# Scores of a gated recurrent branch: float32 products replaced by three products of rounded high and low parts, in a two-block transformer kernel

## The chip, the cores and the metric

The kernel is one program on one core of a Trainium2 chip. The metric is device time in microseconds (us) of the whole program. Its engines are TensorE (PE in the profile; PEld is its weight load), VectorE (DVE), ScalarE (ACT), GpSimd (POOL) and SyncE (SP), which issues most transfers.

## The reference, cut to what matters

The first of two blocks has two layers (`l` = 0, 1) over 256 context tokens and 256 latent tokens. Each layer has three branches. The first, A, is a gated linear-attention recurrence with 4 heads, 128 wide in queries and keys and 256 wide in values, run forwards and backwards. In one chunk of the reference:

```python
qh = heads(q, A_QK)
kh = heads(k, A_QK) * (A_QK ** -0.5)
a = jnp.exp(dmat - m_row[..., None]) * jnp.einsum('bhtd,bhsd->bhts', qc, kc)
num = jnp.einsum('bhts,bhsv->bhtv', a, vc) + ...
den = jnp.sum(a, axis=-1) + ...
h = num / jnp.maximum(jnp.abs(den), jnp.exp(-m_row))[..., None]
```

The change touches only how `q k^T` is multiplied. Everything is float32 in the reference.

## The kernel before

**Split products.** Nearly all matrix products of the kernel are made as three products of rounded parts: x = high + low, where high is x rounded to the type `fp32r` and low is x - high rounded to it, and xy is taken as high·high + high·low + low·high (`mm3`). Weights arrive by DMA in units of up to 128x2048 in `raw`. ScalarE writes the high part of a unit (`wh`), in a first piece of 1280 and a second of 768 columns, and VectorE writes the low part (`wl`) in the same two pieces. In the code this conversion is `used(tag, j)`: it converts the unit two turns later in the order, because there are two buffers, and it can start only when TensorE has finished the unit that it replaces. So `used("a_qk", ...)` stands behind the keys' projection.

**Branch A.** Tokens lie in four tiles of 128. Layer 0 computes all four (N = 512 queries); layer 1 computes the last two (N = 256 queries) against all 512 keys. For head `h` TensorE goes through, in this order:

- the query projection into PSUM bank 0 and the key projection into bank 1 (`queries`, `keys`; for head 0, `first_units`);
- at heads 0 and 2, values of two heads (`values_of`), tile by tile into banks 0, 1, 2, 3 (head 0 of layer 1: banks 4, 5, 0, 1);
- turning the output of the head before (`outputs_turned`), and at odd heads the first half of the output gate (`o_gate(h, (0,))`, bank 0);
- the scores, one product per tile of queries into banks 4 to 7: 256 keys for tiles 0 and 1, 512 keys for tiles 2 and 3. They are plain float32 products of `a_qk`;
- the rest of the output gate, the `z` gate, the turning of the weighted scores (`turns`) and the product with the values (`outs`).

ScalarE copies bank 0 and bank 1 to `a_qk` (events `a_q`, `a_k`), and its copy of the keys carries the scale. These copies also free the banks: `values_of` and `o_gate` wait for them. Scores of layer 0 wait besides for the end of the previous head's output on VectorE (`a_y`).

**VectorE's order.** Each engine runs its instructions strictly in the order written. At the end of a head, VectorE does `root`, `diagonals(h + 1)`, the low part of the unit behind `a_qk` (`used`), `outputs(l, h)` and then, in the next head, the score multiplications (`tensor_tensor_reduce`). Before head 0 it makes the gates' running sums: a memset, six scans, four small operations (event `a_rc`). ScalarE then stores the factors to memory and reads them back spread over all partitions (`factors_stored`, `factors_spread`), VectorE adds them up in `diagonals(0)`, ScalarE takes the exponentials (`exponentials(0)`) and, in layer 0, only then copies the values out of banks 0 to 3 (event `a_v`). The first output gate of layer 0 waits for that copy, because it writes bank 0.

Of the kernel before, what the change touches and what calls it, by code (L numbers as in the profile page):

```python
# [11 lines left out]
ALU = mybir.AluOpType  # L12
ACT = mybir.ActivationFunctionType
# [208 lines left out]
def program(nc, wpk, xin, memt, vec, tabs, tabs2, rpb, out):  # L222
# [13 lines left out]
    with ctx:  # L236
# [3 lines left out]
        def signal(name):  # L240
            return Signal(name, ctx.enter_context(nc.semaphore(name)))
# [31 lines left out]
        act_step = signal("act_step")  # L273
        lo_split = signal("lo_split")
        dve_step = signal("dve_step")
# [27 lines left out]
        def tm(off, shape):  # L303
            n = int(np.prod(shape))
            v = TM[:, off:off + n]
            if len(shape) == 2:
                v = v.rearrange("p (a b) -> p a b", a=shape[0])
            elif len(shape) == 3:
                v = v.rearrange("p (a b c) -> p a b c", a=shape[0], b=shape[1])
            return v  # L310

        def bank(b):
            return PS[:, b]
# [4 lines left out]
        def hy(base, kn, n):  # L318

            parts = HY[:, :, base:base + kn * n].rearrange("p s (k t) -> p s k t", k=kn)  # L320
            return parts[:, 0], parts[:, 1], parts
# [43 lines left out]
        YB = hy(4096, 8, 512)  # L365
# [16 lines left out]
        GROUPS = ((0, 0), (1, 256))  # L382


        a_qk, a_f, a_b = tm(0, [2, 512]), tm(2048, [4, 512]), tm(4096, [4, 512])
        a_v, a_v_pair = [tm(o, [4, 256]) for o in (1024, 6144)], tm(0, [2, 5120])[:, :, 1024:2048]
        a_dirs = (a_f, a_b)
        a_g, a_z, a_h, a_rr = tm(7168, [2, 512]), tm(8192, [2, 512]), tm(9216, [4, 256]), tm(9216, [2, 512])
# [259 lines left out]
        def tensor_program(P):  # L648
            free = {}

            def mm(o, l, r, start=True, stop=True):
                return P.x.matmul(o, l, r, start=start, stop=stop)  # L652
# [156 lines left out]
            def branch_a(l):  # L809
                t0, N = lay(l)  # L810
# [36 lines left out]
                def values_of(h, half, tiles):  # L847
                    u = place["a_v", 4 * l + h + half]
                    w, v = weights(u)
                    for i in tiles:  # L850
                        o = a_v_bank(l, h, i)
                        if half == 0 and o < 2:
                            P.wait_ge(act_step, (("a_q", "a_k")[o], l, h))
                        elif half == 0 and o == 2 and h == 0:
                            P.wait_ge(act_step, ("a_gt", l))
                        for k in range(4):
                            split_done(u, k)
                            P.wait_ge(*ready(4 * half + k))
                            t = mm3(bank(o), H[0][:, 4 * half + k, 128 * i:128 * i + 128], H[1][:, 4 * half + k, 128 * i:128 * i + 128],
                                    w[:, k], v[:, k], half == 0 and k == 0, half == 1 and k == 3)  # L860
                        if half or i == 3:
                            t.then_inc(*projected.mark(*([("a_v", l, h, i)] if half else []), *([("unit", u)] if i == 3 else [])))
# [21 lines left out]
                def o_gate(h, cs):  # L884
                    u = place["a_o", 4 * l + h]
                    for c in cs:
                        if h % 2:
                            P.wait_ge(act_step, (("a_q", "a_k")[c], l, h))
                        else:
                            P.wait_ge(act_step, ("a_v", l, h, c + 2 if l and h == 0 else c))  # L890
                        proj_t(bank(c)[:, 0:N], u, 128 * c, 128, H, ready, 0, 8, t0, N, ("a_o", l, h, c), *([("unit", u)] if c else []))
# [21 lines left out]
                for h in range(4):  # L913
                    if h % 2:
                        o_gate(h, (0,))
                    P.wait_ge(act_step, ("a_k", l, h))
                    if h == 0:
                        P.wait_ge(act_step, ("a_cm", l))
                    elif l == 0:
                        P.wait_ge(dve_step, ("a_y", l, h - 1, 1))  # L920
                    for i in range(i0, 4):
                        n = a_keys(i)
                        mm(bank(4 + i)[:, 0:n], a_qk[:, 0, 128 * i:128 * i + 128], a_qk[:, 1, 0:n]).then_inc(
                            *pe_step.mark(("a_s", l, h, i)))
                    o_gate(h, (1,) if h % 2 else (0, 1))
                    u = place["a_z", 4 * l + h]
                    for c in range(2):
                        P.wait_ge(act_step, ("a_o", l, h, c))
                        proj_t(bank(c)[:, 0:N], u, 128 * c, 128, H, ready, 0, 8, t0, N, ("a_z", l, h, c), *([("unit", u)] if c else []))
                        if c == 0:  # L930
                            turns(h)
                    outs(h)
                    if h < 3:
                        queries(h + 1)
                        keys(h + 1)
                        if h == 1:
                            values_of(2, 0, (0, 1))
                        outputs_turned(l, h)
                    if h == 1:
                        values_of(2, 0, (2, 3))  # L940
                        values_of(2, 1, range(4))
# [819 lines left out]
        def scalar_program(A):  # L1761
            def act(o, i, f, *events, **kw):
                return A.x.activation(o, i, f, **kw).then_inc(*act_step.mark(*events))  # L1763
# [59 lines left out]
            def branch_a(l):  # L1823
                t0, N = lay(l)
# [18 lines left out]

                def queries(h):
                    A.wait_ge(projected, ("a_q", l, h))
                    act(a_qk[:, 0, t0:512], bank(0)[:, 0:N], ACT.Copy, ("a_q", l, h))

                def keys(h):
                    A.wait_ge(projected, ("a_k", l, h))
                    act(a_qk[:, 1], bank(1), ACT.Copy, ("a_k", l, h), scale=128.0 ** -0.5)  # L1850
                    used("a_qk", 4 * l + h)

                def values_of(h, tiles):
# [647 lines left out]
            for l in range(2):  # L2501
                t0, N = lay(l)
# [38 lines left out]
        def vector_program(D):  # L2541
            def tt(o, a, b, op, *events):
                return D.x.tensor_tensor(o, a, b, op).then_inc(*dve_step.mark(*events))  # L2543
# [6 lines left out]
            def stt(o, a, s, b, op0, op1, *events):  # L2550
                return D.x.scalar_tensor_tensor(out=o, in0=a, scalar=s, in1=b, op0=op0, op1=op1).then_inc(*dve_step.mark(*events))  # L2551
# [14 lines left out]
            def used(tag, j):  # L2566
                convert(unit_after(place[tag, j]))
# [78 lines left out]
            def ada_turn(q):  # L2646
                l, j = divmod(ada_content(q), 12)
                D.wait_ge(pe_step, ("ada_turned", q))
                groups = bank(turn_bank(q))[:, 0:256].rearrange("p (h g c) -> p h c g", h=2, g=4)[:, :, 0:2]
                D.x.reduce_sum(group_sums, groups, AX).then_inc(*dve_step.mark())  # L2650
                D.wait_own(dve_step)
                tt(ada[:, l, 2 * j:2 * j + 2, :], group_sums, vcol(f"bada{l}", 2 * j, 2).unsqueeze(2).to_broadcast([128, 2, 2]), ALU.add, ("ada", q))
# [43 lines left out]
            def branch_a(l):  # L2696
                t0, N = lay(l)
                i0 = t0 // 128
                used("gate", l)
                if l:  # L2700
                    used("a_qk", 4)
                    ada_turn(23)
                D.wait_ge(act_step, ("a_ln", l))
                stt(a_g[:, 1], a_gt, 0.0, a_g[:, 0], ALU.min, ALU.subtract)
                D.wait_own(dve_step)
                cp(a_fg[0], a_g[64:68, 1])
                cp(a_fg[1], a_g[96:100, 1])
                D.x.memset(a_z[:, 1], 0.0).then_inc(*dve_step.mark())
                D.wait_own(dve_step)

                def scan(o, a, b, init, op):
# [21 lines left out]
                def diagonals(h):  # L2733
                    if h:
                        D.wait_ge(pe_step, ("a_turned", l, h - 1, 3))
                    D.wait_ge(factors_in[h % 2], (l, h))
                    for d in range(2):
                        for i in range(i0, 4):
                            a0 = 128 * i
                            stt(a_dirs[d][:, i, a0:a0 + 128], a_factor(d, h)[:, a0:a0 + 128], a_col(d, i, h), a_masks[d],  # L2740
                                ALU.add, ALU.add, ("a_diag", l, h, d))

                diagonals(0)
                for h in range(4):
# [51 lines left out]
                    root(colS[:, 28 + i0:32], colS[:, 20 + i0:24], colS[:, 24 + i0:28], ("a_root", l, h), eps=64 * EPS)  # L2796
                    if h < 3:
                        diagonals(h + 1)
                        used("a_qk", 4 * l + h + 1)
                        outputs(l, h)  # L2800
                        if h == 1:
                            outputs_low(l, 1)

# [6 lines left out]
            def outputs(l, h):  # L2810
                t0, N = lay(l)
                for c in range(2):
                    D.wait_ge(pe_step, ("a_yt", l, h, c))
                    stt(a_z[:, c, 0:N], bank(4 + c)[:, 0:N], vcol(f"anw{l}", 2 * h + c), a_g[:, c, 0:N], ALU.mult, ALU.mult, ("a_y", l, h, c))
# [1131 lines left out]
```

## Time and profile before

| | us |
|---|---|
| median of 3 runs | 2233.77 (2231.61 to 2234.32) |
| the profiled execution | 2233.6 |
| its span, first to last instruction | 2231.6 |
| PE busy | 2208.0 (99%) |
| PE weight loads busy | 1955.8 (88%) |
| DVE busy | 1367.8 (61%) |
| ACT busy | 1046.8 (47%) |
| POOL busy | 275.1 (12%) |

Busy time is the union of an engine's instructions. The times of single rows below count from the first instruction of the span. A matmul's row lasts longer than its turn on the engine, as successive ones overlap: the step from one start to the next is what it costs.

### The profile page before, as it was taken

The page shows a single profiled execution, that of the slowest core. Times are in us where ns is not written, and L with a number is a line of the kernel's source. Part 1 is how long each engine was busy: PE and PEld are TensorE (multiplying, and loading weights), DVE is VectorE, ACT ScalarE, POOL GpSimd, SP SyncE. Part 2 cuts the span into 40 slices and gives each one's busy share as a digit, 9 for nine tenths or more (in the row PEclk, how much of TensorE's full clock was granted, in tenths as well). Part 3 has the DMA queues.
Part 4 walks back from the last instruction along what each step waited for, and adds up shares of the span by engine and source line. Part 5 has one row for each costly group of instructions (what it writes and reads, how often), then busy time and mean ns, then how long its engine had stood idle before and what let it go on. Part 6 is the DMA issues. An engine that isn't in the chain of part 4 may idle for free.

```text
span 2231.6 us, 35053 instructions
## 1 busy us (share of the span) xinstructions
PE 2208.0 (99%) x14494; PEld 1955.8 (88%) x14494; DVE 1367.8 (61%) x2620; ACT 1046.8 (47%) x1994; POOL 275.1 (12%) x299
## 2 busy tenths in 40 slices
PE   8999999999999999999999999999999999999998
PEld 7888878999978888878899999999888888988887
DVE  6644523577755243467465776557777876667875
ACT  5543422345442233354443556445466554566553
POOL 0000000222201032100002220120210110110110
PEclk9999999999999999999999999999999999999999
DMA  8522234221234222235343223446433555334544
GB/s 314 185 96 77 76 151 170 77 77 58 77 107 141 93 78 93 85 132 172 112 151 133 79 93 114 178 166 218 147 124 136 190 178 191 119 107 142 186 174 147
DMA packets 55535, 298.09 MB, mean 134 GB/s; under 512 B 9344, under 2 KB 16256, under 8 KB 24208
## 3 DMA queue, kind: packets, MB, share of 16 engines
q1 hardware_dynamic: 53040, 291.62, 37.0%
q10 hardware_dynamic: 2336, 4.23, 0.7%
q8 instruction: 114, 1.87, 0.3%
q14 instruction: 45, 0.37, 0.0%
HBM read 292.65 MB, written 3.44 MB: 133 GB/s over the span
## 4 chain that ended last, share of the span: by engine, by line
PE 90%; DVE 6%; ACT 2%; DMA 1%; issue 1%; POOL 0%; SPq 0%; DVEq 0%; ACTq 0%
PE PS L652 86%; PE PS L656 3%; DVE TM L2543 1%; DVE wl L2562 1%; ACT TM L1763 1%; ACT TMG L1763 0%; DVE wl L2564 0%; DVE colS L2551 0%; DVE colS L3146 0%; ACT wh L1773 0%; DMA raw<-in_wpk 0%; DVE TMG L2551 0%; DMA Y<-factors_d 0%; DVE HY L2551 0%; ACT HY L1763 0%
## 5 line engine op out<-in xcount | busy, mean ns | idle before, releaser
L652 PE MATMUL PS<-HY,wh 128*128 128x512 f32 (+3 forms) x4944 | 1282.3, 343 | 5.8 <-DVE TM L2551 1.7
L652 PEld LDWEIGHTS PS<-HY,wh 128*128 128x128 f32 (+2 forms) x4944 | 847.9, 189 | 122.3 <-issue 9.4
L652 PE MATMUL PS<-HY,wl 128*128 128x256 f32 (+1 forms) x3000 | 925.2, 308 | 0.0
L652 PEld LDWEIGHTS PS<-HY,wl 128*128 128x128 f32 x3000 | 566.8, 189 | 30.0
L2562 DVE TENSOR_TENSOR wl<-raw,wh 128x1280 fp32r<-128x1280 f32 (+1 forms) x238 | 346.9, 1458 | 362.8 <-ACT wh L1773 362.7
L652 PE MATMUL PS<-wh,HY 128*128 128x256 f32 (+1 forms) x2468 | 527.3, 306 | 0.2
L1763 ACT ACTIVATE TM<-PS 128x512 f32<-128x512 f32 (+4 forms) x375 | 184.2, 500 | 520.1 <-PE PS L652 416.9
L652 PEld LDWEIGHTS PS<-wh,HY 128*128 128x128 f32 x2468 | 405.8, 191 | 19.7 <-ACT TM L1763 0.8
L1773 ACT ACTIVATE wh<-raw 128x1280 fp32r<-128x1280 f32 (+2 forms) x246 | 295.8, 1202 | 243.6 <-PE PS L652 171.8
L652 PE MATMUL PS<-wl,HY 128*128 128x256 f32 (+1 forms) x1234 | 373.4, 303 | 0.0
L2564 DVE TENSOR_TENSOR wl<-raw,wh 128x768 fp32r<-128x768 f32 (+1 forms) x238 | 249.8, 1049 | 0.0
L652 PEld LDWEIGHTS PS<-wl,HY 128*128 128x128 f32 x1234 | 236.1, 191 | 8.6
L1774 ACT ACTIVATE wh<-raw 128x768 fp32r<-128x768 f32 (+2 forms) x246 | 200.2, 814 | 0.0
L3518 POOL TENSOR_TENSOR HY<-TM,HY 128x256 fp32r<-128x256 f32 (+2 forms) x64 | 62.7, 981 | 351.2 <-ACT HY L1763 350.3
L1763 ACT ACTIVATE TMG<-PS 128x512 f32<-128x512 f32 (+2 forms) x113 | 49.3, 457 | 105.9 <-PE PS L652 98.6
L2543 DVE TENSOR_TENSOR TM<-PS,TM 128x512 f32<-128x512 f32 (+3 forms) x92 | 47.6, 545 | 72.5 <-ACT TM L1763 70.2
L1763 ACT ACTIVATE TMG<-PS,colS 128x512 f32<-128x512 f32 (+1 forms) x108 | 63.9, 599 | 57.0 <-DVE colS L2547 56.4
L652 PE MATMUL PS<-TM 128*128 128x128 f32 (+4 forms) x512 | 86.7, 331 | 1.0 <-ACT TM L1763 0.7
L3518 POOL TENSOR_TENSOR TM<-TM,wtab 128x256 f32<-128x256 f32 x64 | 68.2, 1086 | 74.1 <-DVE colS L2907 67.6
L3518 POOL TENSOR_TENSOR TM<-TM,T 128x512 f32<-128x512 f32 (+2 forms) x30 | 30.9, 1046 | 371.3 <-PE PS L652 188.9
L652 PEld LDWEIGHTS PS<-TM 128*128 128x128 f32 (+2 forms) x512 | 65.9, 190 | 9.4 <-issue 5.0
L1763 ACT ACTIVATE HY<-TM 128x256 fp32r<-128x256 f32 (+2 forms) x82 | 42.1, 520 | 60.2 <-POOL TM L3518 31.5
(198 smaller groups left out, 1798.7 us busy)
## 6 DMA issues: line engine op xcount, KB each, us to landing
raw<-in_wpk SPq DMA_DIRECT2D x233, 1024.0 KB, 4.8
raw<-in_wpk SPq DMA_DIRECT2D x32, 704.0 KB, 4.0
TM<-in_wpk SPq DMA_DIRECT2D x6, 1024.0 KB, 16.7
Y<-factors_d ACTq DMA_DIRECT2D x16, 256.0 KB, 5.5
X<-in_xin SPq DMA_DIRECT2D x1, 2048.0 KB, 15.3
Y<-in_wpk SPq DMA_DIRECT2D x2, 1024.0 KB, 20.5
Y<-bias_d SPq DMA_DIRECT2D x4, 512.0 KB, 10.2
raw<-in_wpk SPq DMA_DIRECT2D x3, 512.0 KB, 3.7
```

The lines of the kernel that those rows point to most:

```text
L652: return P.x.matmul(o, l, r, start=start, stop=stop)
L656: return P.x.transpose(o, i, ident[0:p, 0:p])
L1763: return A.x.activation(o, i, f, **kw).then_inc(*act_step.mark(*events))
L1773: A.x.activation(wh[:, s, 0:c], raw[:, r, 0:c], ACT.Copy).then_inc(*hi_split.mark((u, 0)))
L1774: A.x.activation(wh[:, s, c:n], raw[:, r, c:n], ACT.Copy).then_inc(*hi_split.mark((u, 1)))
L2543: return D.x.tensor_tensor(o, a, b, op).then_inc(*dve_step.mark(*events))
L2562: D.x.tensor_tensor(wl[:, s, 0:c], raw[:, r, 0:c], wh[:, s, 0:c], ALU.subtract).then_inc(*lo_split.mark((u, 0)))
L2564: D.x.tensor_tensor(wl[:, s, c:n], raw[:, r, c:n], wh[:, s, c:n], ALU.subtract).then_inc(*lo_split.mark(u))
L3518: return G.x.tensor_tensor(o, a, b, op).then_inc(*pool_step.mark(*events))
```

## The change

Queries and keys of branch A are no longer kept as float32 in `a_qk`. ScalarE's two copies now write rounded high parts into a slice of the `fp32r` buffer `YB` (`a_high(0)` for queries, `a_high(1)` for keys), and VectorE makes the low parts (`a_low`) from the PSUM banks and the high parts: `low_queries` one tensor-tensor subtraction, `low_keys` one scalar-tensor-tensor operation with the scale. Each score product becomes three. What waited for ScalarE's copies in order to overwrite banks 0 and 1 now waits for the low parts, and the scores wait for both low parts. VectorE's new operations stand: for head 0 ahead of the gate work (layer 1) or ahead of the scans (layer 0); for later heads, the queries' behind `diagonals(h + 1)`, and the keys' behind the conversion `used("a_qk", ...)` at h + 1 = 2, and behind `outputs(l, h)` as well at h + 1 = 1 and 3.

```diff
-        a_qk, a_f, a_b = tm(0, [2, 512]), tm(2048, [4, 512]), tm(4096, [4, 512])
+        a_f, a_b = tm(2048, [4, 512]), tm(4096, [4, 512])
+
+        def a_high(c):
+            return YB[c][:, 6]
+
+        def a_low(c):
+            return YB[c][:, 7]
...
                         if half == 0 and o < 2:
-                            P.wait_ge(act_step, (("a_q", "a_k")[o], l, h))
+                            P.wait_ge(dve_step, ("a_low", l, h, o))
...
                         if h % 2:
-                            P.wait_ge(act_step, (("a_q", "a_k")[c], l, h))
+                            P.wait_ge(dve_step, ("a_low", l, h, c))
...
                     P.wait_ge(act_step, ("a_k", l, h))
+                    P.wait_ge(dve_step, ("a_low", l, h, 0), ("a_low", l, h, 1))
...
-                        mm(bank(4 + i)[:, 0:n], a_qk[:, 0, 128 * i:128 * i + 128], a_qk[:, 1, 0:n]).then_inc(
+                        own = slice(128 * i, 128 * i + 128)
+                        mm3(bank(4 + i)[:, 0:n], a_high(0)[:, own], a_low(0)[:, own], a_high(1)[:, 0:n], a_low(1)[:, 0:n], True, True).then_inc(
                             *pe_step.mark(("a_s", l, h, i)))
...
-                    act(a_qk[:, 0, t0:512], bank(0)[:, 0:N], ACT.Copy, ("a_q", l, h))
+                    act(a_high(0)[:, t0:512], bank(0)[:, 0:N], ACT.Copy, ("a_q", l, h))
...
-                    act(a_qk[:, 1], bank(1), ACT.Copy, ("a_k", l, h), scale=128.0 ** -0.5)
+                    act(a_high(1), bank(1), ACT.Copy, ("a_k", l, h), scale=128.0 ** -0.5)
                     used("a_qk", 4 * l + h)
...
+                def low_queries(h):
+                    D.wait_ge(act_step, ("a_q", l, h))
+                    tt(a_low(0)[:, t0:512], bank(0)[:, 0:N], a_high(0)[:, t0:512], ALU.subtract, ("a_low", l, h, 0))
+
+                def low_keys(h):
+                    D.wait_ge(act_step, ("a_k", l, h))
+                    stt(a_low(1), bank(1), 128.0 ** -0.5, a_high(1), ALU.mult, ALU.subtract, ("a_low", l, h, 1))
+
+                if l:
+                    low_queries(0)
+                    low_keys(0)
                 D.wait_ge(act_step, ("a_ln", l))
...
                 D.x.memset(a_z[:, 1], 0.0).then_inc(*dve_step.mark())
+                if l == 0:
+                    low_queries(0)
+                    low_keys(0)
                 D.wait_own(dve_step)
...
                         diagonals(h + 1)
+                        low_queries(h + 1)
                         used("a_qk", 4 * l + h + 1)
+                        if h == 1:
+                            low_keys(h + 1)
                         outputs(l, h)
+                        if h != 1:
+                            low_keys(h + 1)
```

## Rows read from the trace of the kernel before

**Rows 1.** The page: TensorE's granted clock in 40 slices, 9 for 90% or more.

```profile
PEclk9999999999999999999999999999999999999999
```

**Rows 2.** The page: the chain of work that ended last, by engine.

```profile
PE 90%; DVE 6%; ACT 2%; DMA 1%; issue 1%; POOL 0%; SPq 0%; DVEq 0%; ACTq 0%
```

**Rows 3.** Timeline, float32 scores, layer 0 head 0: start, us, engine, line, operation.

```profile
97.19 2.74 PE L652 MATMUL PS<-TM 128*128 128x256 f32 x8
...
99.77 0.19 PEld L652 LDWEIGHTS PS<-HY,wh 128*128 128x128 f32 x1 [0.24 <-issue]
```

**Rows 4.** Timeline, TensorE: split products 512 and 256 columns wide.

```profile
182.56 0.39 PE L652 MATMUL PS<-wl,HY 128*128 128x512 f32 x1
...
183.24 0.39 PE L652 MATMUL PS<-wl,HY 128*128 128x512 f32 x1
...
1041.39 0.28 PE L652 MATMUL PS<-HY,wl 128*128 128x256 f32 x1
...
1041.75 0.28 PE L652 MATMUL PS<-HY,wl 128*128 128x256 f32 x1
```

**Rows 5.** Timeline, layer 0, VectorE's outputs ahead of the scores of head 1, and the scores.

```profile
143.24 1.41 DVE L2551 SCALAR_TENSOR_TENSOR TM<-PS,V,TM 128x512 f32<-128x512 f32 x2
...
145.32 2.74 PE L652 MATMUL PS<-TM 128*128 128x256 f32 x8
```

**Rows 6.** Timeline, layer 0 before and at head 0: weight loads, ScalarE, VectorE.

```profile
73.52 1.28 ACT L1763 ACTIVATE TM<-PS 128x512 f32<-128x512 f32 x2 [3.21 <-PE PS L652]
...
74.17 0.19 PEld L652 LDWEIGHTS PS<-wh,HY 128*128 128x128 f32 x1 [0.43 <-ACT TM L1763]
74.28 0.19 PEld L652 LDWEIGHTS PS<-wl,HY 128*128 128x128 f32 x1
...
72.63 1.21 DVE L2712 TENSOR_TENSOR_SCAN TM<-TM 4x512 f32<-4x512 f32 x1
...
80.18 0.67 DVE L2543 TENSOR_TENSOR rows<-TMG,TM 4x512 f32<-4x512 f32 x1
...
82.90 2.13 ACTq L1842 DMA_DIRECT2D Y<-factors_d  x4
...
92.46 2.19 DVE L2551 SCALAR_TENSOR_TENSOR TM<-Y,colC,T 128x128 f32<-128x128 f32 x8 [5.62 <-DMA Y<-factors_d]
...
98.32 2.07 ACT L1763 ACTIVATE TM<-PS 128x512 f32<-128x512 f32 x4 [0.89 <-ACT TM L1763]
```

**Rows 7.** Timeline, layer 0, keys of head 2 and the values behind them.

```profile
181.66 0.39 PE L652 MATMUL PS<-wh,HY 128*128 128x512 f32 x1
...
184.15 0.61 PE L652 MATMUL PS<-wh,HY 128*128 128x512 f32 x2
...
181.85 0.60 ACT L1763 ACTIVATE TM<-PS 128x512 f32<-128x512 f32 x1 [1.23 <-PE PS L652]
...
185.06 0.95 DVE L2564 TENSOR_TENSOR wl<-raw,wh 128x768 fp32r<-128x768 f32 x1
```

**Rows 8.** Timeline, layer 1, keys and scores of head 1.

```profile
1042.95 1.88 PE L652 MATMUL PS<-TM 128*128 128x512 f32 x4
...
1043.91 0.87 DVE L2551 SCALAR_TENSOR_TENSOR TM<-PS,V,TM 128x256 f32<-128x256 f32 x2
1044.70 0.55 DVE L2756 CUSTOM_DVE_ANT_0 TM<-PS,TM 128x384 f32<-128x384 f32 x1
```

**Rows 9.** Timeline, layer 1, TensorE at the gates of head 0.

```profile
1023.82 1.32 PE L656 MATMUL PS<-T,TM 128*128 128x128 f32 x8 [0.20 <-DVE TM L2551]
```

**Rows 10.** Windows at the end of the span: TensorE busy (instructions), granted clock, DMA share, GB/s.

```profile
2226.00:2228.00 2.00, 0.00 (x1) 1.00 0.16 54
2228.00:2230.00 2.00, 0.00 (x0) 0.64 1.03 340
```

**Rows 11.** Waits of TensorE from 1140 us to the end: us, times, longest; 9 rows, first and last.

```profile
PE PS L652 <- DVE TM L2551: 1.7, 1, 1.7
...
PE PS L656 <- DVE colS L2551: 0.2, 1, 0.2
```

## The prediction

> **What bounds the kernel now.** I read the page first, for the bound: the chain that ended last is TensorE for 90% of the span [rows 2], and its granted clock is full in every slice [rows 1]. So an edit counts in two ways only: by the time that its own products take on TensorE, and by the time that TensorE is held at a wait. Then I read timelines around the eight places where scores are made (four heads in each of two layers), to see what TensorE does in the moments in which it will have to wait for VectorE. The question at each place: when does the new low part come, and when does TensorE want it?
>
> **What the products save.** Eight matmul records make the four float32 scores of a head of layer 0. They begin at 97.19, and the weight load that starts with the first gate product's turn is at 99.77 [rows 3]: 2.58 us for 256+256+512+512 columns, or 1.68 ns a column, so 0.86 for 512 and 0.43 for 256. Split products step by 0.68 us for three at 512 columns (182.56 to 183.24) and by 0.36 for three at 256 (1041.39 to 1041.75) [rows 4]. A head of layer 0 then takes 2×0.68 + 2×0.36 = 2.08: 0.50 less. A head of layer 1, with two products of 512, takes 1.36 instead of 1.72: 0.36 less. All eight heads: 3.4 us. That is all that can be won, and less than the 4.5 us (0.2%) that a measurement of this kernel can tell from no change.
>
> **What is added.** ScalarE's copies stay as they are, with another output. VectorE gets sixteen operations. The nearest price is two operations of 128x512 with a PSUM operand in 1.41 us, 0.70 each [rows 5]; the writing to the rounded type is not shown with a PSUM operand, so I bound it from both sides: not under half of that, 0.35, as the data are the same, and not over twice, 1.4. I take 0.70. VectorE has the time. What matters is that it works in order, and what stands ahead of the keys' low part. One more price: a wait that truly holds TensorE also stops its weight loads from running ahead. At 74.17 a load was released and the next one started at 74.28 [rows 6], so the first product begins 0.11 after its release.
>
> **Values of heads 2 (once in each layer), the first large cost.** The first tile of values goes to bank 0 from 181.66; the second starts at 184.38, the second product of the row at 184.15 (0.23 later) [rows 7], and it goes to bank 1. It used to need ScalarE's copy of the keys, which starts at 181.85 and takes 0.60 [rows 7]: long done. Now it needs `low_keys`, and ahead of that on VectorE stands the conversion of the unit whose buffer the keys' projection has only just left: ScalarE rounds it behind the copy, VectorE follows, and its last piece runs from 185.06 for 0.95 [rows 7]. So `low_keys` runs from 186.01 to 186.71, the product starts at 186.82, and TensorE is held 2.44 us. In layer 1 the same chain stands behind the same product, with the same distances. Two places: 4.9. Behind the held product stand TensorE's whole queue and all that follows it; nothing takes up the time.
>
> **Scores of heads 1 and 3 in layer 1, the second.** They begin at 1042.95 and waited for no VectorE result. The conversion and both outputs now stand ahead of `low_keys`: the outputs begin at 1043.91, and what followed them began at 1044.70 [rows 8]. So `low_keys` ends at 1045.40, the scores start at 1045.51, and TensorE is held 2.56. The pattern repeats at head 3. Two places: 5.1. The score multiplications that began at 1044.70 shift by less than TensorE does, so no second wait comes of it.
>
> **Scores of heads 1 and 3 in layer 0.** Here N is twice as large and covers it: the outputs run from 143.24 for 1.41, `low_keys` would end at 145.35, and the scores began at 145.32 [rows 5]. With the 0.11, 0.14 at most; I take 0.1, twice: 0.2.
>
> **Head 0 of layer 0.** Two things. The first tile of values was released at 74.17 by the copy of the queries [rows 6] and now waits 0.70 more for `low_queries`. And the scans: they started at 72.63, while TensorE was still projecting; now they stand behind `low_keys`, which waits for the copy of the keys (73.52 + 1.28 = 74.80 [rows 6]) and ends at 75.5. The scans, the factors (last operation at 80.18), the store, the spreading read (issued from 82.90) and the sums that wait for it (92.46, idle until the transfer landed) all move by 2.9 [rows 6]. ScalarE works without a pause worth the name from there to its copies of the values, whose first starts at 98.32 [rows 6] and, with the 0.60 of such a copy [rows 7], ends at 98.92. Moved, 101.82; with the 0.11, 101.93. The first gate began at 99.77 [rows 3] and needs that bank, so it is late by 2.16. This is counted from before, so the 0.70 and the head's own saving are in it.
>
> **Head 0 of layer 1.** VectorE's two operations stand where it waits for ScalarE, and two other tiles go first, so I cost them at nothing; without that cover they would cost up to 1.4. But its saving of 0.36 is lost too: soon after these scores TensorE waits for VectorE's weights (0.20 at 1023.82 [rows 9]), which hang on the spread factors and not on TensorE, and it would only wait longer.
>
> **The sum.** Held: 2.16 + 4.88 + 5.12 + 0.2 = 12.4. Saved: 3×0.50 + 3×0.36 = 2.6. Net +9.8. On the profiled execution's 2233.6 (the median of the runs is 2233.77, the same for this purpose) that is 2243.4.
>
> **Rival 1: the factors are not late.** The spreading read takes long: issued from 82.90, the last that counts landed before 92.46, 9.6 us on [rows 6], beside a weight unit on the same engines. Moved by 2.9, it could meet less traffic and land relatively earlier. For it: the lag is long. Against it: that unit is released by VectorE's next conversion, which moves by the same amount. If all 2.9 are regained, the first gate is late only by 0.70 - 0.50 = 0.2, the net is 7.8 and the time 2241.4. Chance 0.08.
>
> **Rival 2: the clock falls in the new pauses.** TensorE has no pause of over 1.7 us in the later part of the run [rows 11], and its clock, 2.4 GHz, is full throughout [rows 1]. After its last work, which ended by 2226.00, it did nothing more, and in the window from 2228 to 2230 the mean granted clock is 0.64, on the way to 1.2 GHz [rows 10]. The four long pauses, 2.3 to 2.5 us, lie between what these rows show at full clock and what they show at its fall. If it fell, the products behind would go at half speed for a while; I bound that by nothing and by two lengths of the pause, so 0 to 2.4 us lost each time. One fall: up to 2245.8; four: up to 2253. Chance of at least one: 0.12. The Trainium skill ("TensorE: Matmul & The Clock Gate", HAM oscillation) says that an engine which idles between bursts is throttled and must work its way back to full rate. By that rule these pauses, not the waits alone, would be the cost; the trace shows full rate through its longest pause, and so I keep the sum without it.
>
> **Rival 3, the other side: the time is given back later, and no change can be measured.** While TensorE is held, ScalarE, VectorE and the transfers could get ahead, and TensorE's later waits would shrink. From 1140 us on there are nine kinds of them, from 1.7 down to 0.2 and 6.3 us in all [rows 11]. If all went, the net is 3.5, and the time 2237.1, within 4.5 of before; it decides from 5.3 of the 6.3. Against it: such waits are steps of dependent chains (a sum, its root, its spreading) that begin with TensorE's own product and so move with it. Chance 0.06.
>
> **How the numbers follow.** Forecast 0.70, rivals 0.08, 0.12 and 0.06; 0.04 is left for what I do not see, half of it for a score product that runs better than the rows say, so that the kernel is faster. The likeliest case has its own range: the VectorE operation at 0.35 takes about 0.35 off each of the five large terms, at 1.4 it adds 0.7 to each, and near 0.7 it is well supported; 2241.5 to 2246. The range of 8 in 10 takes in rival 1 and one fall of the clock: 2240 to 2248. Slower: 0.70 + 0.08 + 0.12 + 0.01 = 0.91; within 0.2%: 0.06 + 0.01 = 0.07; faster 0.02.
>
> **What would show each step.** In the profile after: three split products per score at 0.68 and 0.36 us; TensorE idle, put down to VectorE, about 2.4 us in the middle of the values of head 2 in both layers and about 2.5 before the scores of heads 1 and 3 in layer 1; the scans of layer 0 starting near 75.5 and the first gate near 101.9, put down to ScalarE; no wait before the scores of layer 0's heads 1 and 3 beyond 0.14; the granted clock at full in all slices. The prediction is wrong if `low_keys` takes much more or less than 0.70, if the clock falls, or if the factors land early.

## The result, and the profile after

| | before | changed |
|---|---|---|
| median, us | 2233.85 (2231.61 to 2236.65, 6 runs) | 2244.28 (2242.84 to 2247.2, 6 runs) |
| ratio | | 1.0053 [1.0043, 1.0063] |
| the profiled execution, its span | 2233.6, 2231.6 | 2247.2, 2245.4 |

The changed kernel is slower by 10.4 us (2244.28 − 2233.85); 9.8 were forecast (2243.4 us). Its profiled execution is the slowest of its six runs, 13.6 over before's, so the trace below has some 3 us more to explain than the median.

The page of the changed kernel: busy times, and the chain that ended last, by engine. They answer to [rows 2].

```profile
PE 2211.1 (98%) x14518; PEld 1962.8 (87%) x14518; DVE 1378.3 (61%) x2636; ACT 1046.9 (47%) x1994; POOL 274.0 (12%) x299
...
PE 88%; DVE 7%; ACT 3%; DMA 1%; issue 1%; ACTq 0%; POOL 0%; SPq 0%; DVEq 0%
```

VectorE is busy 10.5 us more than before and TensorE 3 us more, and the chain has moved 2% of the span from TensorE to VectorE and ScalarE. The clock line of its page is that of [rows 1], 9 everywhere, which says only that no slice of 56 us fell below 90%: a fall of a few microseconds does not show in it. Where TensorE waits says more.

TensorE's waits in the changed kernel between 60 and 1160 us (total us, times, longest):

```profile
PE PS L659 <- DVE HY L2560: 5.3, 5, 2.1
PE PS L659 <- ACT HY L1772: 4.8, 2, 2.4
...
PE PS L659 <- DVE HY L2552: 0.7, 1, 0.7
```

The first line has two waits of 2.1 us for `low_keys` (line 2560 writing `HY`) among its five; the other three, 1.0 us in all, wait for other work of that line and were there before. The last is `low_queries` of head 0. The second line looks like ScalarE, and the timeline shows that it is not.

Timelines of the changed kernel, layer 1, VectorE, ScalarE and TensorE around the scores of head 1 (they answer to [rows 8]):

```profile
1048.57 0.95 DVE L2573 TENSOR_TENSOR wl<-raw,wh 128x768 fp32r<-128x768 f32 x1
1049.44 0.87 DVE L2560 SCALAR_TENSOR_TENSOR TM<-PS,V,TM 128x256 f32<-128x256 f32 x2
1050.23 0.68 DVE L2560 SCALAR_TENSOR_TENSOR HY<-PS,HY 128x512 fp32r<-128x512 f32 x1
...
1050.34 0.63 ACT L1772 ACTIVATE HY<-TM 128x512 fp32r<-128x512 f32 x1 [2.48 <-DVE TM L2560]
...
1048.36 0.28 PE L659 MATMUL PS<-HY,wl 128*128 128x256 f32 x1
1051.05 2.30 PE L659 MATMUL PS<-HY 128*128 128x512 f32 x6 [2.42 <-ACT HY L1772]
```

In this order VectorE makes the second piece of a weight unit, two outputs, and only then `low_keys`, which ends at 1050.91. The score products wait for `low_keys` by the program. ScalarE's copy of the outputs, to another part of `HY`, happens to end at 1050.97, 0.06 later, and the profile puts a wait down to what ended last. TensorE was to begin at 1048.48 (1048.36 plus the step of 0.12) and begins at 1051.05: 2.57 us held.

The same for the values of head 2 in layer 0 (they answer to [rows 7]):

```profile
185.87 0.95 DVE L2573 TENSOR_TENSOR wl<-raw,wh 128x768 fp32r<-128x768 f32 x1
186.74 0.68 DVE L2560 SCALAR_TENSOR_TENSOR HY<-PS,HY 128x512 fp32r<-128x512 f32 x1
...
184.96 0.39 PE L659 MATMUL PS<-wh,HY 128*128 128x512 f32 x1
187.47 0.50 PE L659 MATMUL PS<-wh,HY 128*128 128x512 f32 x1 [2.13 <-DVE HY L2560]
187.81 0.39 PE L659 MATMUL PS<-wl,HY 128*128 128x512 f32 x1
...
188.76 0.63 PE L659 MATMUL PS<-wl,HY 128*128 128x512 f32 x1
190.04 0.63 PE L659 MATMUL PS<-wl,HY 128*128 128x512 f32 x1
```

Without a wait the next product would begin at 185.19. It is released at 187.47, and the product behind it starts 0.34 later instead of 0.23, so the first itself begins at 187.58: held 2.39 us. The same `x6 [2.42` comes back at 1131.42, and the same 2.13 at 1080.35: four pauses, as foreseen. The last two rows were not foreseen as the likely course: from one product with `wl` to the next is 1.28 us instead of 0.68 [rows 4].

TensorE in five stretches of the changed kernel: stretch, us, busy (matmuls), mean granted clock, DMA share, GB/s. The first four us of work behind each of the four pauses, and the stretch around 975.

```profile
188.00:192.00 4.00, 4.00 (x12) 0.57 0.68 247
973.00:977.00 4.00, 4.00 (x24) 0.57 0.41 172
1051.00:1055.00 4.00, 3.95 (x15) 0.60 0.57 231
1080.00:1084.00 4.00, 3.65 (x18) 1.00 0.74 262
1131.00:1135.00 4.00, 3.58 (x24) 1.00 0.65 246
```

The clock is at 1.2 GHz for most of the first three stretches and at 2.4 GHz in the last two. So two of the four pauses of this execution were followed by a fall, two were not, and one fall, at 973, stands behind no long pause. Before the change no slice of the page fell below 90% [rows 1], and windows of its trace from 60 to 1160 and from 1160 to 2226 us have a mean of 1.00.

Head 0 of layer 0, VectorE, ScalarE, TensorE (they answer to [rows 6] and [rows 3]):

```profile
74.98 0.69 DVE L2560 SCALAR_TENSOR_TENSOR HY<-PS,HY 128x512 fp32r<-128x512 f32 x1
75.71 1.21 DVE L2736 TENSOR_TENSOR_SCAN TM<-TM 4x512 f32<-4x512 f32 x1
...
94.33 2.19 DVE L2560 SCALAR_TENSOR_TENSOR TM<-Y,colC,T 128x128 f32<-128x128 f32 x8 [6.62 <-DMA Y<-factors_d]
...
85.76 1.85 ACTq L1851 DMA_DIRECT2D Y<-factors_d  x4
...
100.84 0.73 PE L659 MATMUL PS<-HY,wh 128*128 128x512 f32 x2 [0.53 <-ACT TM L1772]
```

The scans start late by 3.1 us and the read is issued late by 2.86, but the sums that wait for it start late by only 1.87: 8.57 us lie between them, against 9.56 before. The gate's second weight load, which stood at 99.77 before [rows 3], is at 100.94: late by 1.17, where 2.16 were forecast. The other profiles of kernels with this order (experiments 1 to 4) have 8.64 to 9.12 us between the two, and the gate late by 1.1 to 1.8.

**The ledger of this trace** compares the start of the same product in both traces, in us: first gate +1.17; held values of heads 2, 2×2.4; held scores of heads 1 and 3 of layer 1, 2×2.57; the saving and small waits of the other heads, −2.3; the clock falls at 188 and 1051, 1.6 each, and at 973, 0.5; and 1.1 at 842, told below. That makes 13.6, and the last product is late by 13.7.

### The profile page after: what moved, and what is told of

Same layout as the page of the kernel before. It is cut to its first block, busy times and chain, and to the rows that moved or that the text cites. A ratio compares the mean times of both kernels' runs of the same rounds, so it can differ in the third digit from the quotient of the medians.

```text
span 2245.4 us, 35118 instructions
## 1 busy us (share of the span) xinstructions
PE 2211.1 (98%) x14518; PEld 1962.8 (87%) x14518; DVE 1378.3 (61%) x2636; ACT 1046.9 (47%) x1994; POOL 274.0 (12%) x299
## 3 DMA queue, kind: packets, MB, share of 16 engines
q8 instruction: 114, 1.87, 0.3%
## 4 chain that ended last, share of the span: by engine, by line
PE 88%; DVE 7%; ACT 3%; DMA 1%; issue 1%; ACTq 0%; POOL 0%; SPq 0%; DVEq 0%
PE PS L659 84%; PE PS L663 3%; DVE TM L2552 1%; DVE wl L2571 1%; ACT TM L1772 1%; DVE wl L2573 1%; DMA Y<-factors_d 1%; ACT wh L1782 1%; ACT TMG L1772 0%; DVE TM L2736 0%; ACT HY L1772 0%; DVE colS L3175 0%; DVE colS L2560 0%; DMA raw<-in_wpk 0%; DVE HY L2560 0%
## 5 line engine op out<-in xcount | busy, mean ns | idle before, releaser
L1772 ACT ACTIVATE TM<-PS 128x512 f32<-128x512 f32 (+3 forms) x359 | 175.5, 498 | 505.1 <-PE PS L659 403.5
L2552 DVE TENSOR_TENSOR TM<-TM 128x256 f32<-128x256 f32 (+7 forms) x146 | 65.7, 465 | 5.9 <-POOL TM L3547 1.2
L659 PE MATMUL PS<-TM 128*128 128x128 f32 (+3 forms) x464 | 68.2, 312 | 1.0 <-ACT TM L1772 0.7
```

## The experiments

Every kernel is compared with runs of the kernel before in its own group. Experiments 1, 2, 3 and the ten products of 4 were run in one group (before: median 2234.13 of 18 runs), the others in a second (2232.81 of 15). The changed kernel itself was run in the second, and in the first measurement above (before: 2233.85), but not in the first group. Line numbers of helpers move by some lines between kernels.

**1. The low part of the keys at the head of the queue.** Products, copies and waits stay as changed; heads 1 to 3 lose their place behind the weight conversion and the outputs.

```diff
                         low_queries(h + 1)
+                        low_keys(h + 1)
                         used("a_qk", 4 * l + h + 1)
-                        if h == 1:
-                            low_keys(h + 1)
                         outputs(l, h)
-                        if h != 1:
-                            low_keys(h + 1)
```

> The changed kernel with one move: VectorE makes the keys' low part right behind the queries', ahead of the conversion of the next weights and of the outputs, at heads 1 to 3. Theory A (the cost is the place of the keys' low part in VectorE's order): the four pauses of about 2.5 us go, and with them every fall of the clock; what is left is head 0 of layer 0 (+1.2) less the savings of the other heads (2.2 to 2.6), so 2232 to 2233.5, the time of the kernel before or 1 us less. Theory B (the split products themselves, or VectorE's added work, cost the time): still 2241 to 2244.

Measured: 2232.11 us (2230.08 to 2233.75, 11 runs), ratio 0.9992 [0.9983, 1.0001]. Its VectorE at head 2 of layer 0:

```profile
183.39 0.69 DVE L2560 SCALAR_TENSOR_TENSOR HY<-PS,HY 128x512 fp32r<-128x512 f32 x1 [4.75 <-ACT HY L1772]
184.55 1.49 DVE L2571 TENSOR_TENSOR wl<-raw,wh 128x1280 fp32r<-128x1280 f32 x1 [0.47 <-ACT wh L1782]
```

`low_keys` now runs while VectorE would wait for ScalarE anyway: the conversion behind it still waits 0.47 us for its high part, so the move costs nothing. In its trace all four long pauses and all falls of the clock are gone, and in its time the whole loss. The cause of the slowdown is the place in VectorE's queue, not the arithmetic.

**2. Only half of that move:** `low_keys` ahead of the conversion for head 2 alone.

```diff
                         low_queries(h + 1)
-                        used("a_qk", 4 * l + h + 1)
                         if h == 1:
                             low_keys(h + 1)
+                        used("a_qk", 4 * l + h + 1)
                         outputs(l, h)
```

> The changed kernel with the keys' low part ahead of the conversion at head 2 alone, in both layers; heads 1 and 3 as changed. Theory A: the two pauses within the values go (2 x 2.45 = 4.9 us) with any fall of the clock behind them, and the two before the scores of layer 1 stay: 2238 to 2240. Theory B: no change, 2243 to 2244. Theory C (a pause costs mostly by the clock): over 6 us less, 2237 or under.

Measured: 2239.63 us (2236.58 to 2241.82, 7 runs), ratio 1.0026 [1.0015, 1.0036]. Its waits of TensorE, 60 to 1160 us:

```profile
PE PS L659 <- ACT HY L1772: 4.8, 2, 2.4
...
PE PS L659 <- DVE HY L2560: 1.6, 4, 0.5
```

The two pauses of 2.42 before the scores stay, those of 2.13 in the values are gone, and the time is 5.5 us over that of before, where the changed kernel's was 10.4: 4.9 come back, as the forecast's two terms say. The other half, from here to experiment 1, is 7.5 us (2239.63 - 2232.11) where they say 5.1. In the two traces it is 4.8 at 1120 us, near the forecast. The excess of 2.4 in the medians stays open. In this trace the clock is full behind both remaining pauses, but three of the seven runs have a mean granted clock of 0.998 or 0.997, so some of it may be falls.

**3. The waits without the new products.** The copies write float32 `a_qk` again and the scores are float32 products; the low parts are made (as PSUM minus `a_qk`) and waited for as in the change, but not used.

```diff
-                        mm3(bank(4 + i)[:, 0:n], a_high(0)[:, own], a_low(0)[:, own], a_high(1)[:, 0:n], a_low(1)[:, 0:n], True, True).then_inc(
+                        mm(bank(4 + i)[:, 0:n], a_qk[:, 0, own], a_qk[:, 1, 0:n]).then_inc(
...
-                    act(a_high(0)[:, t0:512], bank(0)[:, 0:N], ACT.Copy, ("a_q", l, h))
+                    act(a_qk[:, 0, t0:512], bank(0)[:, 0:N], ACT.Copy, ("a_q", l, h))
...
-                    act(a_high(1), bank(1), ACT.Copy, ("a_k", l, h), scale=128.0 ** -0.5)
+                    act(a_qk[:, 1], bank(1), ACT.Copy, ("a_k", l, h), scale=128.0 ** -0.5)
```

> The changed kernel with its added VectorE work and all its waits, but with scores as float32 products of float32 queries and keys as in the kernel before. The low parts are made and not used (they come out as differences of equal numbers). It isolates what the products save. Theory A: the products save 0.50 us a head in layer 0 and 0.36 in layer 1, so the time is 2 to 3 us over the changed kernel's, 2246 to 2247. Theory B (the split products cost as much as they save, or more): equal to the changed kernel or faster, 2242 to 2244.

Measured: 2247.05 us (2245.4 to 2250.83, 4 runs), ratio 1.0062 [1.0048, 1.0076]. That is 12.9 over before in its group, where the changed kernel was 10.4 over in the first measurement: 2.5 for what the products save, and the sum had 2.6. The intervals of the two ratios overlap, so the times alone do not show it; the rows do. Its scores of head 2 of layer 0, and beneath them those of the changed kernel:

```profile
210.06 2.74 PE L659 MATMUL PS<-TM 128*128 128x256 f32 x8
```

```profile
209.14 2.26 PE L659 MATMUL PS<-HY 128*128 128x256 f32 x12
211.24 0.62 PE L659 MATMUL PS<-HY,wh 128*128 128x512 f32 x2
```

Eight records against twelve, and in the changed kernel 2.10 us from their start to the gate's, where 2.58 were needed before [rows 3]. The products do what they were to do.

**4. The pauses filled, and the changed kernel again.** Ten products of the identity with itself, 128 columns wide, into a PSUM bank not in use there, ahead of each of the four long waits; then a second variant with eight, together with the changed kernel itself. The waits stay; only TensorE is no longer idle.

```diff
                         o = a_v_bank(l, h, i)
+                        if h == 2 and half == 0 and o == 1:
+                            keep(10, 7)
...
                     P.wait_ge(act_step, ("a_k", l, h))
+                    if l and h % 2:
+                        keep(10, 7)
                     P.wait_ge(dve_step, ("a_low", l, h, 0), ("a_low", l, h, 1))
```

> The changed kernel with the four long pauses filled: TensorE makes ten products of the identity with itself (about 2.2 us, into bank 7, overwritten later) ahead of each of the four waits. The waits end when they did. Theory C (part of the cost is the clock, which falls in or soon after a pause): granted clock 1.0 through the span, no half-rate stretch, times near 2242.8 to 2243 in every run and closer together than the 2242.8 to 2247.2 of the changed kernel. Theory A alone (a pause costs its length and no more): the same times as the changed kernel, 2244, or a little over.

> The changed kernel with eight products of the identity (about 1.8 us) ahead of each of the four long waits, instead of ten. The fill is sure to end before the wait does. Theory C (clock falls add to the typical time): no fall in the trace and a median 1 to 2 us under the changed kernel's in the same rounds. Rival (the falls are rare enough, or the spread comes from elsewhere): the same median as the changed kernel's within 0.5 us, and a spread as wide.

> The changed kernel as it is, on the same chip and in the same rounds as the others of this call. To be compared with the filled kernel, and to see in one more trace how often the clock falls. Queue theory: the same four pauses, 2.13, 2.42, 2.13 and 2.42 us, whatever the clock does. If the clock adds to the cost, the times spread over 2242.8 to 2247 as before, with a fall or more in the slower ones.

| kernel | us | ratio |
|---|---|---|
| ten products | 2246.34 (2241.52 to 2247.02, 5 runs) | 1.0050 [1.0038, 1.0063] |
| eight products | 2244.86 (2244.39 to 2245.95, 5 runs) | 1.0056 [1.0044, 1.0069] |
| changed, again | 2245.08 (2242.91 to 2246.57, 5 runs) | 1.0055 [1.0041, 1.0069] |

The kernel with eight: TensorE at the first pause, and two stretches of 260 us that hold all four pauses.

```profile
185.10 1.95 PE L659 MATMUL PS<-T 128*128 128x128 f32 x16
187.38 0.50 PE L659 MATMUL PS<-wh,HY 128*128 128x512 f32 x1 [0.33 <-DVE HY L2564]
```

```profile
60.00:320.00 260.00, 258.34 (x1246) 1.00 0.32 109
900.00:1160.00 260.00, 256.11 (x1527) 1.00 0.36 121
```

The idle time of 2.13 became 0.33, the first held product still begins at the same place, and the clock is full in both stretches. The changed kernel beside it fell three times, once at each of the other three pauses:

```profile
1051.00:1055.00 4.00, 4.00 (x21) 0.68 0.47 197
1081.00:1085.00 4.00, 4.00 (x14) 0.59 0.49 205
1132.00:1136.00 4.00, 3.75 (x13) 0.57 0.63 246
```

Two of these falls begin in the last 0.2 us of a pause, at 1050.2 and 1132.1; the others of the changed kernel begin 0.7 to 1.3 us behind a pause. In all traces here a long pause can let the clock fall, and no filled one did.

What a fall costs shows where branch A ends. The product that started at 1119.46 before, in the changed kernel's first profile and in the kernel with eight:

```profile
1133.23 0.40 PE L659 MATMUL PS<-HY,wh 128*128 128x256 f32 x2
```

```profile
1129.44 0.40 PE L659 MATMUL PS<-HY,wh 128*128 128x256 f32 x2
```

It is late by 13.8 with three falls and by 10.0 with none. In the changed kernel's second profile it is late by 16.1, with ten products by 9.9. So up to there the filled kernels are 3.8 to 6.2 us ahead of the unfilled one, although the four waits ended when they did; some 1 us of the larger figure is a longer wait of the second profile at the first gate of layer 1 (told in experiment 5).

But the medians did not follow: 0.2 us apart with eight, and with ten the kernel was no faster either. I had expected 1 to 2 us. Nor does the spread tell anything: 1.6 us with eight and 5.5 with ten, against 3.7 for the changed kernel. All ten filled runs have a mean granted clock of 0.999 or 1.0, so falls do not spread them. Between 1120 us and the end the delay changes by -3.1 to +0.9 us from trace to trace, by other causes (see the two paces below), and that is as much as the falls cost.

In this group the changed kernel lies 12.3 us over before, in the first measurement 10.4.

**5. Both moves.** Experiment 1, and for head 0 of layer 0 the two low parts behind the first scan instead of ahead of it.

```diff
-                if l == 0:
-                    low_queries(0)
-                    low_keys(0)
                 D.wait_own(dve_step)
...
                 scan(a_bs[0], a_fg[0], a_zero[0], 0.0, ALU.add)
+                if l == 0:
+                    low_queries(0)
+                    low_keys(0)
                 scan(a_m[0], a_fg[0], a_i[0], 0.0, ALU.max)
```

> The keys' low part ahead of the conversion at heads 1 to 3, and head 0 of layer 0 reordered as well: both low parts stand behind the first scan instead of ahead of all six. The first scan then runs while VectorE waited for the keys' copy, and the factors move by about 1.8 us instead of 3.0. By the queue theory the first gate of layer 0 then starts near 100.1 instead of 100.8 to 101.1, and nearly the whole saving of the products is kept: 0.8 us less than with the first move alone, 2231 to 2231.5, against 2234 before. By its rival (the gate waits for the transfers, which take their own time) the gate stays at 100.8 to 101 and the time at 2232.

Measured: 2232.95 us (2228.59 to 2235.33, 11 runs), ratio 0.9997 [0.9989, 1.0006]. Its timelines: VectorE, and TensorE at the first gate of layer 0 and of layer 1.

```profile
72.74 1.21 DVE L2733 TENSOR_TENSOR_SCAN TM<-TM 4x512 f32<-4x512 f32 x1
74.33 0.69 DVE L2552 TENSOR_TENSOR HY<-PS,HY 128x512 fp32r<-128x512 f32 x1 [0.38 <-ACT HY L1772]
...
100.22 0.62 PE L659 MATMUL PS<-HY,wh 128*128 128x512 f32 x2
...
1021.12 0.51 PE L659 MATMUL PS<-HY,wh 128*128 128x256 f32 x2 [2.23 <-ACT TM L1772]
```

The first scan fills the time in which VectorE waited for ScalarE, and the first gate of layer 0 no longer waits, as expected. In layer 1, where nothing was altered for head 0, the same gate waited 2.23 us in this execution, 0.53 in the changed kernel's and 1.60 in its second profile: from the issue of the spreading read to the sums are 8.84, 6.91 and 8.21 us. The time missed its forecast of 2231 to 2231.5, and the gain of 0.8 us on experiment 1 did not show: against before in its own group, experiment 1 is at -2.0 us and this one at +0.1. No version here is shown to be faster than before.

**6. The keys' low part made twice.** First into scratch, then into its place: one more VectorE operation of the same size ahead of each release.

```diff
+                    stt(tm(0, [512]), bank(1), 128.0 ** -0.5, a_high(1), ALU.mult, ALU.subtract)
                     stt(a_low(1), bank(1), 128.0 ** -0.5, a_high(1), ALU.mult, ALU.subtract, ("a_low", l, h, 1))
```

> The changed kernel with the operation of the keys' low part made twice, once into unused space and then as before. Queue theory: 0.69 us more at each place where this operation ends a wait: the two within the values, the two before the scores of layer 1, the two before the scores of layer 0's heads 1 and 3 (whose margin was used up) and, through the scans, the first gate of layer 0. Seven places, 4.8 us over the changed kernel, about 2249. Rival (only the four long pauses lie on the path): 2.8 us more, 2247.

Measured: 2252.47 us (2249.72 to 2254.86, 4 runs), ratio 1.0089 [1.0075, 1.0103]: 7.4 more than the changed kernel beside it. Timelines of VectorE and TensorE, and a window of the third fall:

```profile
188.13 0.68 DVE L2560 SCALAR_TENSOR_TENSOR TM<-PS,HY 128x512 f32<-128x512 f32 x1
188.73 0.68 DVE L2560 SCALAR_TENSOR_TENSOR HY<-PS,HY 128x512 fp32r<-128x512 f32 x1
...
189.46 0.79 PE L659 MATMUL PS<-wh,HY 128*128 128x512 f32 x1 [2.73 <-DVE HY L2560]
```

```profile
1134.00:1142.00 8.00, 6.74 (x28) 0.57 0.38 131
```

The two start 0.60 apart, and the four pauses are 2.73, 3.02, 2.73 and 3.02: each longer by 0.60, the whole of what was put ahead of them. The same operation also delays the gate of head 0 of layer 0 and the scores of heads 1 and 3 there, about 0.6 each; seven places make 4.2, where 4.8 were expected. The other 3.2 are not explained by the queue. The trace has three falls of the clock, one of which lasts twice as long as any in the changed kernel: 8 us at a mean of 0.57. The four runs have a mean granted clock of 0.996 or 0.997, the five of the changed kernel beside them 0.997 to 0.999. Falls may account for the rest; it is not shown.

## Why the prediction held, and where it did not

- **The products save.** Forecast 2.08 and 1.36 us a head, 0.50 and 0.36 less. Measured 2.10 and 1.36. Experiment 3 gives 2.5 for all, forecast 2.6, within a wide interval.
- **The operation costs 0.70.** Measured 0.68 to 0.69: writing the rounded type from PSUM costs nothing extra (experiment 6 has the same operation with either output, 0.68 both).
- **Values of heads 2, 2.44 each.** Measured 2.4 twice. The place behind the weight conversion is the cause (experiments 1 and 2).
- **Scores of heads 1 and 3 of layer 1, 2.56 each.** Measured 2.57 and 2.58. Experiment 6 shows that what is put ahead of the release comes out whole at TensorE.
- **Scores of heads 1 and 3 of layer 0, 0.1 each.** The saving of head 1 moved the delay from 1.17 only to 0.84, so 0.50 less 0.33: about 0.17 was held. It is a margin: with 0.60 more on VectorE the profile of experiment 6 has a wait of 0.51 there.
- **Head 0 of layer 1.** Its 0.36 was lost, as forecast, but not at the place named: the wait of 0.20 for VectorE behind the gates [rows 9] is still 0.20. The first gate's wait for ScalarE's copy grew from 0.19 (at 1020.48 before) to 0.53. The delay fell from 5.56 to 5.18 at the scores and was back at 5.53 at the gate.
- **The first gate of layer 0, 2.16: mis-sized.** Measured 1.17, and 1.1 to 1.8 over the seven profiles with this order. The step that failed is that the read takes the 9.56 us of the trace before and so moves by what its issue moves; it took 8.57. That is rival 1 in outcome, for a third of its 2.9, but its reason (less traffic in the way) is not shown: in experiment 5 the read was issued only 1.45 late and took 8.76, and before has one trace, in which the read may have been a long one.
- **Rival 2, the clock, was set too low.** Given 0.12 for a single fall or more, it came about in the profiles of the changed kernel both times, three falls each. Its price was bounded by 2.4 us each and is 1.6 at 188 and 1051. Of the 18 pauses of 2.1 to 3.0 us in five traces (the changed kernel twice, experiments 2, 3 and 6) eleven had a fall in them or up to 1.4 us behind, and seven passed without one; none of the eight filled pauses had one. The step that failed is "the trace shows full rate through its longest pause": that was 1.7 us in the stretch looked at, and it said nothing on 2.4. The Trainium skill ("TensorE: Matmul & The Clock Gate", HAM oscillation) says that an engine that idles between bursts loses its full clock. The traces agree, for about half of the pauses.
- **Rival 3, given back later,** did not happen: past 1160 us TensorE's waits are the same nine kinds as before, 6.3 us in all, and the delay is as large at the end (13.7) as at 1133 (13.8).

The sum without the gate's error is 9.8 − 1.0 = 8.8. Without the falls (3.7) and the 1.1 at 842 the ledger of the trace is 8.8 too, and the lowest run, 2242.84, lies 9.0 over before's median. The median lies 10.4 over it, and 12.3 in the second group. So the forecast time is close partly by luck: a term too large by 1.0 stood in for falls of the clock that were left out.

The mean granted clock of every run says how common falls are. The eleven runs of the changed kernel have 0.999 in two, the two fastest (2242.84 and 2242.91); 0.998 in five (2243.9 to 2246.57); and 0.997 in four (2245.08 to 2247.2), among them both profiled ones with three falls each. Of the 33 runs of before in the two groups all but one have 0.999 or 1.0, and of the 22 of experiments 1 and 5 all but three. So a typical run of the changed kernel has falls, and its time goes with them: the median of the eleven, 2244.37, is 1.5 us over the two fastest, and I estimate the price of the falls in it at 1 to 2 us. Against it stand the filled kernels, whose medians are no lower. How much the falls add to the median is therefore not settled.

## What to carry to other kernels

When a value moves from an engine that was early to one that works in order, ask what stands ahead of the new operation in that queue, before asking what it costs: 0.69 us of work cost up to 2.57 at TensorE, and moving the same operation one or two places up cost nothing. A sum of waits tells the mechanism, but the pauses of 2.1 us and more on TensorE needed a term for the clock, of 0 to 1.6 us each in the changed kernel. And a wait's name in the profile is the last to finish; read the program for what it waits for.

## What was not expected of the hardware

**Two paces at full clock.** The same stage of 256-wide split products runs at one of two paces. TensorE in windows of the kernel before, and of the changed one:

```profile
1730.00:1790.00 60.00, 60.00 (x347) 1.00 0.53 191
2060.00:2110.00 50.00, 50.00 (x285) 1.00 0.54 185
```

```profile
1730.00:1790.00 60.00, 60.00 (x341) 1.00 0.51 179
2060.00:2110.00 50.00, 50.00 (x294) 1.00 0.54 190
```

Between the same kinds of work, 347 against 341 matmuls in 60 us and 285 against 294 in 50 us, with TensorE busy and at 2.4 GHz throughout. Along the trace the changed kernel's delay grows from 13.8 to 15.9 us in the first stage and shrinks to 13.7 in the second: 2 us each way. Other kernels' traces have one of the two shifts, both or neither, so it does not go with the change. The cause is open; it can hide what a fall of the clock costs.

**A weight conversion beside GpSimd.** In the changed kernel's trace VectorE and GpSimd at 837:

```profile
838.32 2.05 DVE L2573 TENSOR_TENSOR wl<-raw,wh 128x768 fp32r<-128x768 f32 x1
...
837.08 4.43 POOL L3547 TENSOR_TENSOR TM<-TM 128x512 f32<-128x512 f32 x2 [6.42 <-DVE TM L2552]
```

The piece takes 0.95 us elsewhere and in this place before; TensorE then waited 1.32 us. This came in five of the ten profiles (the changed kernel both times, and experiments 1, 6 and the eight products). That GpSimd works beside it is not enough: before the change the same pair of GpSimd operations starts at 833.14 and the piece at 834.38, 1.24 later as here, and takes 0.95. There GpSimd takes 4.57 us, and 4.42 or 4.43 in the five profiles with the slow piece, so one of the two gives way to the other. What decides which was not tried.

**A fall of the clock without a pause,** at 973, in the changed kernel and in experiment 3. TensorE waited for nothing between 900 and 974 us and is listed busy for the whole of 969 to 973. What stands there are small products, 41 in these 4 us, 16 of them one column wide; the trace shows no other reason.

**A start at the slower pace.** TensorE in two windows of the kernel before, with the same products of 128 columns in both:

```profile
8.00:10.00 2.00, 2.00 (x12) 1.00 1.00 418
10.00:12.00 2.00, 2.00 (x21) 1.00 0.98 398
```

It is busy in both, with 12 products against 21, so up to about 10 us it goes at little more than half the pace, which speaks for 1.2 GHz. The windows and the clock line of the page say full clock there all the same: the profile's clock does not cover this start. Ahead of the first product TensorE had stood still for 3.86 us. Together with the 1.7 us that passed at full clock, this was the nearest that the trace of before had to say on pauses of 2.4.
